# Joined ends between the stages of a two-model kernel on one core: statistics by tile, one Pool product for two, full x from its two parts

## What is computed

```python
# first model, each layer
h = x @ w_in[l]                       # split into 11 parts
y_rwkv, y_mla, y_conv, y_mem = ...    # y_conv: layer norm over channels, y_mla: rms-normed latents @ w_uq, w_ukv
gates = sigmoid(merge + b_gate[l])    # merge is the last part of h
x = layer_norm(ALPHA * x + sum(gates * proj) @ w_out[l], ln_g[l], ln_b[l])
# second model, each layer: three sublayers on x (256 tokens) and on xc (256 context tokens)
x = x + 0.5 * gate * rms_norm(swiglu(modulate(rms_norm(x, g_pre), shift, scale), w1, w2), g_post)
...
p = softmax(scores); o = p @ v        # 6 pairs of heads, queries of 128 tokens
```

## Time and profile before

| | us |
|---|---|
| median of three runs (2942.78 to 2947.43) | 2947.24 |
| the profiled execution | 2938.85 |
| its span, first to last instruction | 2937.0 |
| PE busy | 2760.8 (94%) |
| PE's weight loads | 2301.6 (78%) |
| Pool busy | 1366.4 (47%) |
| DVE busy | 1014.1 (35%) |
| ACT busy | 664.8 (23%) |

### The profile page before, as it was taken

One profiled execution on the slowest core, in us unless ns is written; L12 is line 12 of the kernel. 1 busy time (PEld: TensorE's weight loads), 2 busy tenths in 40 slices (PEclk: granted clock), 3 DMA queues, 4 the chain that ended last, 5 costly groups with the idle time before them and its releaser, 6 DMA issues.

```text
span 2937.0 us, 44510 instructions
## 1 busy us (share of the span) xinstructions
PE 2760.8 (94%) x17649; PEld 2301.6 (78%) x17649; DVE 1014.1 (35%) x1592; ACT 664.8 (23%) x1228; POOL 1366.4 (47%) x626
## 2 busy tenths in 40 slices
PE   8999999999999996999989899999989999796898
PEld 7987777699777865888878668888878888765896
DVE  1742753246337323002341532003330023443237
ACT  3432212144321112000131442001130011334001
POOL 4820000176000003666646764666556666666786
PEclk9999999999999998999999999999999999998999
DMA  6546634444565344222213122222222222321443
GB/s 223 184 182 236 255 147 154 168 172 174 216 247 216 125 158 144 89 97 100 100 58 115 44 64 87 100 97 89 100 86 100 93 92 100 115 73 43 164 170 138
DMA packets 68302, 390.25 MB, mean 133 GB/s; under 512 B 19168, under 2 KB 20800, under 8 KB 21952
## 3 DMA queue, kind: packets, MB, share of 16 engines
q1 hardware_dynamic: 66320, 379.03, 36.0%
q10 hardware_dynamic: 1840, 9.18, 0.9%
HBM read 387.09 MB, written 1.10 MB: 132 GB/s over the span
## 4 chain that ended last, share of the span: by engine, by line
issue 25%; POOL 13%; POOLq 10%; PE 8%; DMA 3%; DVE 1%; SPq 1%; ACT 0%; DVEq 0%; ACTq 0%
POOL m_ws L1722 9%; POOLq L1721 7%; DMA m_ring<-in_panels 3%; POOL m_prob L1756 2%; PE m_bank L1889 2%; POOLq L1734 1%; SPq L1679 1%; PE m_bank L1805 1%; POOL m_ws L1740 1%; PE m_bank L1806 1%; PE m_bank L1807 1%; POOLq L1739 1%; DVE m_ws L2411 1%; PE m_bank L1985 1%; PE m_bank L1987 0%
## 5 line engine op out<-in xcount | busy, mean ns | idle before, releaser
L1805 PE MATMUL m_bank<-m_aT,m_ws 128*128 128x512 f32 (+1 forms) x1792 | 631.1, 352 | 40.9 <-DVE m_aT_low L2379 17.2
L1806 PE MATMUL m_bank<-m_aT_low,m_ws 128*128 128x512 f32 (+1 forms) x1792 | 627.7, 350 | 0.0
L1807 PE MATMUL m_bank<-m_aT,m_ws 128*128 128x512 f32 (+1 forms) x1792 | 627.3, 350 | 0.0
L1722 POOL TENSOR_TENSOR m_ws<-m_ring,m_ws 128x2048 fp32r<-128x2048 f32 x125 | 584.3, 4674 | 18.4
L1889 PE MATMUL m_bank<-m_ws,m_hs 128*128 128x512 f32 x1848 | 422.6, 390 | 3.5 <-DVE m_ws L2411 1.4
L1805 PEld LDWEIGHTS m_bank<-m_aT,m_ws 128*128 128x128 f32 x1792 | 344.8, 192 | 88.5 <-issue 37.7
L1889 PEld LDWEIGHTS m_bank<-m_ws,m_hs 128*128 128x128 f32 x1848 | 346.1, 188 | 79.2 <-issue 6.9
L371 POOL TENSOR_TENSOR m_ws<-m_ring,m_ws 128x2048 fp32r<-128x2048 f32 x48 | 221.5, 4625 | 348.3 <-ACT m_ws L883 348.2
L1806 PEld LDWEIGHTS m_bank<-m_aT_low,m_ws 128*128 128x128 f32 x1792 | 344.8, 192 | 42.3
L1807 PEld LDWEIGHTS m_bank<-m_aT,m_ws 128*128 128x128 f32 x1792 | 344.5, 192 | 42.6
L1733 POOL TENSOR_TENSOR m_small<-m_small 128x1 f32<-128x1 f32 x158 | 33.1, 209 | 583.3 <-PE m_bank L1807 402.0
(11 more groups left out here) (349 smaller groups left out, 3483.5 us busy)
## 6 DMA issues: line engine op xcount, KB each, us to landing
m_ring<-in_panels SPq DMA_DIRECT2D x352, 1024.0 KB, 4.9
m_rows<-m_gg_dram ACTq DMA_DIRECT2D x6, 1024.0 KB, 5.4
m_bias<-in_rpb SPq DMA_DIRECT2D x48, 64.0 KB, 2.7
m_hT<-in_ln_rows ACTq DMA_DIRECT2D x2, 1024.0 KB, 6.9
m_con<-in_con SPq DMA_DIRECT2D x1, 1536.0 KB, 10.6
memT_ctx<-in_memT SPq DMA_DIRECT2D x1, 1024.0 KB, 5.9
x_tok<-in_x SPq DMA_DIRECT2D x1, 1024.0 KB, 13.9
memT_ctx<-in_ctx SPq DMA_DIRECT2D x1, 1024.0 KB, 7.2
```

What stands on the lines that cost most here:

```text
L1722: nc.gpsimd.tensor_tensor(ws[:, p, 1, :], ring[:, p, :], ws[:, p, 0, :].bitcast(F32), ALU.subtract)\
L1805: mm(out, w, a, start=start, stop=False)
L1806: mm(out, w, a_low, start=False, stop=False)
L1807: return mm(out, w_low, a, start=False, stop=stop)
```

## The change

The functions are those above; lines that only renumber a semaphore are left out.

In the first model PE's second transposition of x and ACT's copies go. Pool adds `xT` and `xT_low` into `xF` after the 24 panels. The latent products wait for `var_in` (DVE has read the variance from the bank that they overwrite) and not for the finished norm, and ACT copies the queries ahead of the convolution's four SiLUs. At the layer's end DVE starts on tile 0 when its banks are complete (`out_ps`), subtracts the mean and multiplies by the gain while ACT takes the root, and the last pass multiplies by the factor and adds the shift.

```diff
+                pool.wait_ge(s["panel_used"], l * PANELS1 + PANEL[("in", 23)] + 1)
+                nc.gpsimd.tensor_tensor(xF[:, :, :], xT[:, :, :].bitcast(F32), xT_low[:, :, :].bitcast(F32), ALU.add)\
+                    .then_inc(s["xF_in"], 1)
...
                 pe.wait_ge(s["lat_n_in"], l + 1)
-                transpose_x(2)
-                pe.wait_ge(s["cnorm"], l + 1)
+                pe.wait_ge(s["var_in"], l + 1)
...
+                        pe.wait_ge(s["xF_in"], l + 1)
                     mod_rows(a, 0)
...
-                dve.wait_ge(s["panel_used"], l * PANELS1 + PANELS1)
                 for i in range(NT):
+                    if i == 0:
+                        dve.wait_ge(s["out_ps"], l + 1)
+                    else:
+                        dve.wait_ge(s["panel_used"], l * PANELS1 + PANELS1)
...
                 dve.sem_inc(s["ln_var"], 1)
+                dve.wait_ge(s["rows_in"], 16 * (l + 1))
+                for i in range(NT):
+                    V.scalar_tensor_tensor(yln[:, i, :], yln[:, i, :], small[:, 64 + 2 * i:65 + 2 * i], ln_rows[:, 0:D],
+                                           ALU.subtract, ALU.mult)
                 dve.wait_ge(s["ln_std"], l + 1)
...
                 for i in range(NT):
-                    V.tensor_scalar(yln[:, i, :], yln[:, i, :], small[:, 64 + 2 * i:65 + 2 * i], small[:, 70 + i:71 + i],
-                                    ALU.subtract, ALU.mult)
-                dve.drain()
-                for i in range(NT):
-                    V.tensor_tensor(yln[:, i, :], yln[:, i, :], ln_rows[:, 0:D], ALU.mult)
-                dve.drain()
-                for i in range(NT):
-                    V.tensor_tensor(x_tok[:, i, :], yln[:, i, :], ln_rows[:, D:2 * D], ALU.add)
+                    V.scalar_tensor_tensor(x_tok[:, i, :], yln[:, i, :], small[:, 70 + i:71 + i], ln_rows[:, D:2 * D],
+                                           ALU.mult, ALU.add)
```

```diff
-        SHARED = (DEPTH - 1) * PANELS2 + AT_W1B
+        SHARED = (DEPTH - 1) * PANELS2 + AT_W1B + 2
...
-                for h in range(2):
-                    at = prob[:, n % 3, h * T2:h * T2 + keys]
-                    last = nc.gpsimd.tensor_scalar(at, at, small[:, m + 8 + h:m + 9 + h], None, ALU.mult)
-                last.then_inc(s["norm_in"], 1)
+                at = prob[:, n % 3, :].rearrange("p (h k) -> p h k", h=2)[:, :, 0:keys]
+                nc.gpsimd.tensor_tensor(at, at, small[:, m + 8:m + 10].unsqueeze(2).broadcast_to([P, 2, keys]), ALU.mult)\
+                    .then_inc(s["norm_in"], 1)
...
-                    if n == first + 3:
+                    low = first + (12 if l < DEPTH - 1 else 2)
+                    if n == low:
                         come(out_panel % 2, out_panel // 2 + 1, out_panel - 1)
-                    if first + 3 <= n < first + 7:
+                    if low <= n < low + 8:
...
-                pe.wait_ge(s["xn_in"], IN_TILES[e] + NT * st + NT)
-                for j in range(KD // 2):
-                    for k in (2 * j, 2 * j + 1):
-                        for i in range(NT):
+                for i in range(NT):
+                    pe.wait_ge(s["xn_in"], IN_TILES[e] + NT * st + i + 1)
+                    for j in range(KD // 2):
+                        for k in (2 * j, 2 * j + 1):
...
-                if outs:
-                    square_out(e - 1, 0, last_panel)
+                for i in range(min(outs, NT)):
+                    square_out(e - 1, i, last_panel)
                 if ins:
                     square_in(e, 0)
-                if outs:
-                    square_out(e - 1, 1, last_panel)
+                if outs > NT:
+                    square_out(e - 1, 2, last_panel)
                 if ins:
+                    square_in(e, 1)
                     scaled(e, 0)
-                    square_in(e, 1)
                     scaled(e, 1)
                 if outs > NT:
-                    square_out(e - 1, 2, last_panel)
                     square_out(e - 1, 3, last_panel)
...
-                for i in range(NT):
-                    if outs:
-                        residual(e - 1, i)
-                    if ins:
-                        normed(e, i)
+                for i in range(min(outs, NT)):
+                    branch(e - 1, i)
+                    dve.drain()
+                    added(i)
+                for i in range(NT if ins else 0):
+                    normed(e, i)
                 if outs > NT:
-                    residual(e - 1, 2)
+                    branch(e - 1, 2)
                 if ins:
                     low(e, 0, 0)
                     low(e, 0, 2)
                 if outs > NT:
-                    residual(e - 1, 3)
+                    dve.drain()
+                    added(2)
+                    branch(e - 1, 3)
+                    dve.drain()
+                    added(3)
```

## The result

| | before, us | after, us |
|---|---|---|
| median beside the change (4 runs of each) | 2946.23 | 2872.72 |
| lowest and highest of these | 2942.78, 2947.43 | 2869.62, 2875.91 |
| profiled execution | 2938.85 | 2875.91 |
| its span | 2937.0 | 2874.0 |
| mean granted clock of PE | 0.979 | 0.985 |

The ratio is 0.9752 (95% interval 0.9736 to 0.9769). Two more comparisons, each on one chip, gave 0.9774 (0.9761 to 0.9787) and 0.9757 (0.9744 to 0.9770). The forecast was 2892.2 us in a range of 2879 to 2911: the direction was right, the size was not. From span to span the gain is 63.0 us where the sum had 55.0; from median to median it is 73.5, 65.8 and 72.7 us.

What follows compares the result with a forecast made beforehand. PE, busy 94% of the span, waited mainly for ACT's scaled rows (58.3 us) and Pool's probabilities (18.1 us). Eight terms summed to 55.0 us, taken from the median 2947.24 to give 2892.2 us; range 2879 to 2911.

Steps and rivals of the forecast that it cites:

- attention: Second model's attention: one Pool product at 2.35 us replaces two scaled copies, split moved into eighths; 14.2 us won.
- latent products: First model, twice: PE starts them without transposing x again or waiting for the convolution's norm; 4.9 us won.
- end of layer 0: First model, after layer 0: the shorter norm removes PE's wait for x; 0.3 us won, no more.
- end of layer 1 and start of the second model: Earlier, shorter layer norm, 3.4 us; second model's first low half ready sooner but limited by Pool's first split, 2.5 us.
- four boundaries: Stretches between second-model sublayers with four tiles: reordered ACT and DVE work starts PE 5.3 us sooner each; 21.2 us.
- last boundary: Second model's last boundary: Pool splits the first two panels alone and the same reordering applies; 7.5 us won.
- output: End of kernel: output tile 0 leaves 3.7 us earlier and tile 1 is half the bytes; 1.0 us won.
- Pool slowed by DVE: Rival, attention: Pool's product pays 3.35 us beside DVE, attention loses about 6 us, time 2912 us; 10%.
- Attention bound elsewhere: Rival: ACT or the score chain sets 3.6 us per item, not 3.1; time 2901 us; 10%.
- The half clock taking it back: Rival, four boundaries: half rate falls wholly on products, losing 18 us in all; time about 2910 us; 7%.
- The broadcast form slow: Rival, attention: Pool's broadcast product costs up to 4.7 us, making the kernel slower at 2962.4 us; 3%.
- The ends not doing what they say: Rival: context half or Pool's panels hold PE, 2.5 us per boundary instead of 5.3; time 2903 us; 5%.

Runs made afterwards that it cites:

- list of forms: Changed kernel with a list of Pool operations of several forms behind its last sum, some beside DVE; 2950.86 us, which says nothing of the kernel.
- old_pieces: Changed kernel with each attention's split panel in quarters at items 3 to 6 again, the product kept; ratio 0.9769 to the kernel before.
- repeated traces: Kernel before profiled again (2942.92 us) and changed kernel twice more (2875.68 and 2872.39 us), all unchanged; traces 72.5 and 76.0 us apart.
- before_again: The kernel before, unchanged, timed 11 times with the clock of each execution; 2942.92 us beside 2943.42.
- first_only: The changed first model with the second model of before; 2928.09 us beside 2945.07 for the kernel before, ratio 0.9952.
- one_product: The kernel before with only Pool's normalisation as one product with a broadcast operand; 2928.14 us beside 2944.63, ratio 0.9939.
- old_lists: Changed kernel with ACT's and DVE's lists at the boundaries and the order of PE's transposes put back; 2900.91 us beside 2943.42, ratio 0.9860.
- old_transposes: Changed kernel with PE's boundary transpositions waiting for both tiles and in the old order; one execution, 2876.14 us.

## Why the prediction was wrong

The forecast missed by 2892.2 - 2872.7 = 19.5 us, and two of its steps failed. In the sum it was the price of the broadcast form: Pool's product was taken at 2.35 us and takes 1.89, and attention won 21.1 us and not 14.2. Behind the sum it was the step from one trace to the medians, 11.5 us, and this one is what takes the result out of the range. Point by point, by the first pair of traces:

| term | forecast | traces |
|---|---|---|
| latent products | 4.9 | 5.3 |
| end of layer 0 | 0.3 | 0.4 |
| end of layer 1 and start of the second model | 5.9 | 5.6 |
| four boundaries | 21.2 | 22.8 |
| attention | 14.2 | 21.1 |
| last boundary | 7.5 | 8.8 |
| output | 1.0 | 1.4 |
| x comes earlier, half-clock stretches in the first model | 0 | -2.5 |
| sum | 55.0 | 62.9 (spans: 63.0) |

- **Attention** is the term that was mis-sized: the price of the broadcast form. It was taken at its lower bound, 2.35 us, "since as many elements are read and written as in that row". It takes 1.89 us, quiet and in attention, and the list of forms has 2.34 us where both operands are in memory: the one that is a number repeated costs less. The difference of 0.46 us sits on the edge: with 2.35 Pool needs 3.6 us per item of layer 1 beside an eighth and holds PE's 3.1, with 1.89 it needs 3.12 and doesn't. That is 4 of the 6.9 us; the rest is layer 0, mainly that the context items with the eighths are 0.6 us longer (20.65 to 21.24) and not 2.8. The eighths do cost 1.7 us there (19.50 without them, in `old_pieces`), but the shorter pass gives back 1.1. The lower bound should have been a pass that reads one operand: the earlier trace rows has it at 618 ns for 128x512.
- **The boundaries** came out at 6.0, 5.8, 5.1 and 5.9 us. The working had 5.9 at full clock and took 5.3 to allow for the old half-clock stretch. It did not stay: PE works 3.3 us of a 3.41 us stretch at half rate where it had worked 4.47 us. The third is at 5.1, where the stretch is 6.83 us long and lies on 5.6 us of products. The expected gaps of 1.5 us were 1.3.
- **The start** had the right mechanism: PE waits 3.42 us for Pool's first split, as the earlier trace rows let expect. The norm's end was 4.2 us and not 3.4, and 14.77 us of waiting and not 16 is what was left; half rate over the first products (4.25 us at 0.50) took 2.1 us back. That 5.6 us came out beside a forecast of 5.9 is in part luck: the larger gain and this loss were both unforeseen. The repeated traces have 6.8 and 7.5 us.
- **The last boundary** was right in its parts: 3.6 us for the shared splits, 3.7 for the lists, measured one by one.
- **The latents**, the layer's end and the output were right to 0.4 us. Pool's sum of the two parts took 4.55 us beside PE's products, and nobody waited for it.
- **From the sum to the median** is the second step that failed. With every term as measured the forecast would have been 2947.24 - 63.0 = 2884.2, inside the range. The other 11.5 us are executions: the median of three that I started from was 3.8 us above that of 55 runs (2943.45), and the two traces are a fast execution of before and a slow one of the changed kernel, 6.8 us together; the 0.9 left is between the medians of 4 and of 14 runs. The forecast said that the profiled execution lay 8.4 us below the median, and carried the same 55 us over without asking in what executions differ. The three pairs of traces show it: the four boundaries (22.8, 22.2 and 22.1 us), attention (21.1 each time), the last boundary (8.8, 8.7 and 8.7) and the output (1.4) repeat, and the first model up to the end of its products doesn't (3.2, 10.4 and 13.6). It has one half-clock stretch of 3.41 us before and five after in the first pair, four and three in the second, four and two in the third, each worth 1.7 us at most (half of 3.41, an estimate). From the first pair to the others that is five and six stretches, 8.5 and 10.2 us at most, where the traces differ by 7.2 and 10.4. What stays open is why the first model gains some 3 to 5 us more than the terms for the latents and the layer's end (5.7).
- **The rivals.** Pool slowed by DVE: not in attention (1892 ns the median, 1894 the longest), but 2.7 us and more once DVE reads two operands from memory. Attention bound elsewhere: at PE's own 3.11 us, where the forecast had it. The half clock taking it back: no, PE works 15.2 us at half rate behind the first products of the four boundaries, where it had worked 17.3; only the third has more (5.6 for 4.5). The broadcast form slow: no. The ends not doing what they say: undone, they give back 23.8 us at the four boundaries. The working of the rival that makes the kernel slower has a slip: it puts the eight quarters at 8 us, where its own 2.0 us each make 16. The loss is then 30p - 93, it decides at p = 4.5, and at 4.7 the time is 2954 and not 2962.4.

## What to carry to other kernels

Price a Pool pass by how many operands it streams from memory and by whether it has one operation or two, and measure the form before relying on a neighbour: here 128x1024 elements took 1.2 us as two copies of two operations with constants, 3.0 as two copies of one, and as one product 1.89 with a broadcast operand and 2.34 with one in memory. Where two engines run in the same rhythm, a few tenths of a microsecond per item decide whether the whole excess counts or nothing; work that far out both ways. When an idle time is shortened, count the half rate behind it too, and take the starting time from more than three runs.

## What the runs showed of the hardware that I had not expected

- A copy on Pool scaled by one operation costs 2.4 times the same copy with two: 1487 ns against 617 ns (128x512, constants); with the factor from memory and in the kernel 1563 against 693 ns. The Trainium skill (GPSIMD Engine Reference, section 3.1) gives 769 ns as the best case for one input of 512 elements. The form with two operations is below that here, the form with one at twice it. By that rule two copies (1.54 us by an estimate from it) should have beaten the product; with one operation each they lose to it (3.10 us against 1.89), with two they win (1.39).
- A broadcast operand costs Pool less than a stream: 1.89 us against 2.34 for 128x1024. Beside DVE's products of two operands in memory both are slower, 2.7 to 2.85 and 3.14 us, and a DVE product of that size takes 2.76 and 3.20 us beside them where it takes 1.23 alone. The Trainium skill (GPSIMD Engine Reference, section 8) names this contention, and the trace agrees.
- How long PE ran at half clock went with its idle times at the boundaries. With 5.1 us of idle time, 3.7 us of transposes and 3.9 us of idle time the stretch was 13.65 us long in 19 of 20 boundaries (before, `before_again`, `first_only`, `one_product` and `old_lists`; the other had 3.41 and 6.83). With 1.3, 2.4 and 3.3 us it was 3.41 or 6.83 us, and so it was at the first three with 2.6, 2.0 to 3.3 and 1.5 to 2.4 us (`old_transposes`). Which of these times counts is not told apart here.
